# One merged loop for the HGRN2 layer: projections run in halves between the levels of the decay matrix

## What is computed

```
q, f_logit, i, g = split(rms_norm(h) @ w_in, 4)          # four 1024x1024 projections
f = lb + (1 - lb) * sigmoid(f_logit);  q = silu(q);  k = 1 - f;  v = i
b = cumsum(log f)
scores[t, s] = sum_k q[t,k] * exp(b[t,k] - b[s,k]) * k[s,k]      for s <= t
o = scores @ v      # in chunks with a running state in the reference, which is the same sum
h = h + (rms_norm(o, o_gain) * sigmoid(g)) @ w_out
```

## Time and profile before

| | us |
|---|---|
| median of 3 runs | 3078.87 |
| lowest, highest | 3076.29, 3081.34 |
| the profiled execution | 3075.35 |
| its span | 3073.6 |
| mean granted TensorE clock in the span | 0.969 |
| TensorE busy | 2937.2 (96%) |
| VectorE busy | 1462.0 (48%) |
| ScalarE busy | 1089.2 (35%) |
| GpSimd busy | 206.7 (7%) |

### The profile page before, as it was taken

How to read it: one execution, slowest core, us unless ns; L and a number is a source line. 1 busy time by engine, 2 the same in 40 slices (tenths; PEclk the granted TensorE clock), 3 DMA queues, 4 the chain that set the end, 5 groups by cost and what they waited for, 6 DMA issues and landing times.

```text
span 3073.6 us, 46468 instructions
## 1 busy us (share of the span) xinstructions
PE 2937.2 (96%) x17931; PEld 2548.8 (83%) x17931; DVE 1462.0 (48%) x2048; ACT 1089.2 (35%) x1717; POOL 206.7 (7%) x169
## 2 busy tenths in 40 slices
PE   8999999999999867799999999999999999799998
PEld 7877779999999866699988888887788887588887
DVE  5555545554344566555553444543533334544432
ACT  4333334333243443343332232332344444332222
POOL 1000000000000122210000110110100000200000
PEclk9999989999999877799999999999999999899999
DMA  4221213332343200033333323223211112233332
GB/s 124 52 61 49 61 42 95 90 89 83 95 121 89 61 1 0 0 90 95 89 92 94 104 69 93 78 71 89 83 49 48 48 48 73 65 96 94 90 94 71
DMA packets 419424, 225.54 MB, mean 73 GB/s; under 512 B 7461, under 2 KB 416294, under 8 KB 419222
## 3 DMA queue, kind: packets, MB, share of 16 engines
q1 hardware_dynamic: 416310, 211.45, 23.8%
q0 software_dynamic: 2256, 10.32, 1.1%
q10 hardware_dynamic: 784, 2.75, 0.3%
HBM read 222.36 MB, written 2.13 MB: 73 GB/s over the span
## 4 chain that ended last, share of the span: by engine, by line
PE 90%; DVE 5%; issue 2%; ACT 1%; POOL 1%; DVEq 0%; DMA 0%; ACTq 0%; POOLq 0%
PE ps L432 39%; PE ps L428 33%; PE ps L733 2%; PE ps L944 2%; PE ps L825 2%; PE ps L902 1%; PE ps L965 1%; PE ps L933 1%; PE ps L651 1%; PE ps L735 1%; PE ps L745 1%; PE ps L869 1%; PE ps L838 1%; PE ps L849 1%; PE ps L716 1%
## 5 line engine op out<-in xcount | busy, mean ns | idle before, releaser
L400 DVE TENSOR_TENSOR wl<-raw,wh 128x1024 fp32r<-128x1024 f32 (+2 forms) x421 | 512.9, 1218 | 437.6 <-ACT wh L396 434.1
L396 ACT ACTIVATE wh<-raw 128x1024 fp32r<-128x1024 f32 (+2 forms) x421 | 425.7, 1011 | 758.9 <-PE ps L428 395.4
L432 PE MATMUL ps<-xh,wh 128*128 128x264 f32 x2736 | 565.0, 288 | 7.3 <-DVE xl L461 5.5
L432 PE MATMUL ps<-xl,wh 128*128 128x264 f32 x2736 | 559.0, 286 | 0.0
L432 PE MATMUL ps<-xh,wl 128*128 128x264 f32 x2736 | 558.6, 286 | 0.0
L432 PEld LDWEIGHTS ps<-xh,wh 128*128 128x128 f32 x2736 | 428.5, 189 | 15.6 <-issue 4.1
L432 PEld LDWEIGHTS ps<-xl,wh 128*128 128x128 f32 x2736 | 426.1, 189 | 0.0
L432 PEld LDWEIGHTS ps<-xh,wl 128*128 128x128 f32 x2736 | 425.1, 189 | 0.0
L428 PE MATMUL ps<-xh,wh 128*128 128x512 f32 x976 | 392.3, 402 | 17.7 <-DVE xl L461 13.9
L428 PE MATMUL ps<-xl,wh 128*128 128x512 f32 x976 | 388.6, 398 | 0.0
L428 PE MATMUL ps<-xh,wl 128*128 128x512 f32 x976 | 386.4, 396 | 0.0
(11 more groups left out here) (295 smaller groups left out, 3915.7 us busy)
## 6 DMA issues: line engine op xcount, KB each, us to landing
raw<-in_w_in SPq DMA_DIRECT2D x88, 512.0 KB, 3.8
raw<-in_ffn_w_gate SPq DMA_DIRECT2D x44, 512.0 KB, 3.9
raw<-in_ffn_w_up SPq DMA_DIRECT2D x44, 512.0 KB, 3.8
raw<-in_w_ffn_in SPq DMA_DIRECT2D x44, 512.0 KB, 3.8
raw<-in_fox_w_in SPq DMA_DIRECT2D x33, 512.0 KB, 4.2
raw<-in_hgrn_w_in SPq DMA_DIRECT2D x32, 512.0 KB, 4.0
raw<-in_ffn_w_down SPq DMA_DIRECT2D x32, 448.0 KB, 3.5
raw<-in_ffn_w_down SPq DMA_DIRECT2D x16, 512.0 KB, 3.7
```

The source lines that it names most:

```text
L396: nc.scalar.activation(wh[:, v % 2, 0:nk, :], raw[:, v % RAW_SLOTS, 0:nk, :], ACT.Copy).then_inc(s("w_hi"), 1)
L400: nc.vector.tensor_tensor(wl[:, v % 2, 0:nk, :], raw[:, v % RAW_SLOTS, 0:nk, :], wh[:, v % 2, 0:nk, :].bitcast(F32), ALU.subtract).then_in ...
L432: last = nc.tensor.matmul(ps[:, bank + b, 0:HALF], w[:, slot, kk, :], x[:, k, b * HALF:(b + 1) * HALF], start=first, stop=end_)
```

## The change

Projections and heads become one loop over heads. A prologue of 3 groups (`PH_HGP`) projects f, q and v of head 0; the loop body of head i (`PH_HG`) projects f, q and v of head i+1 and the gate g of head i; the last body (`PH_HGL`) projects head 7's gate, and then does 8 groups of the output projection over the 6 heads that are done by then. `PH_HGOUT` keeps 8 groups over the last 2 heads, of 2 k tiles each. The dense groups of prologue and loop all use the one bank pair 0 and 1, the levels banks 2 and 3 in turn, the off-diagonal scores banks 4 and 5, outputs and the last 16 tokens 7 and 6.

A dense group is cut in two halves of 4 k tiles, and TensorE's order puts something between them or between groups. The diagonal comes first among the levels. Level buffers become three. All distances go to GpSimd. Sigmoids become -|x|, exp, ln(1+.), min and subtract, exp, so that ScalarE needs one table. Picks take only the later halves of the blocks (256 of 512 columns) from level 1 on, the last 16 tokens have their own small picks. `g_o` is no longer copied: the norm and the gate read bank 7.

```diff
-PH_HGRN = Phase(PH_DOWN0, HG_H, K8)
-PH_HGOUT = Phase(PH_HGRN, 2, K8)
+HG_BANKS = (0, 0)
+HG_EARLY = HG_H - 2
+PH_HGP = Phase(PH_DOWN0, 1, [[KT]] * 3, HG_BANKS)
+PH_HG = Phase(PH_HGP, HG_H - 1, K8, HG_BANKS)
+PH_HGL = Phase(PH_HG, 1, [[KT]] + [[HG_EARLY]] * KT, HG_BANKS)
+PH_HGOUT = Phase(PH_HGL, 2, [[KT - HG_EARLY]] * 4, (0, 2) if (PH_HGL.g0 + PH_HGL.gpi) % 2 else (2, 0))
...
     TensorE, body of head i
+        hgrn_level_mm(i, 0); hgrn_level_mm(i, 1)
+        half(0, 0)
+        hgrn_last_tokens(i)
+        if not first(i): hgrn_out(i - 1)
+        half(0, 1)
+        hgrn_level_mm(i, 2); hgrn_level_mm(i, 3)
+        half(1, 0)
+        if not first(i): hgrn_sum(i - 1, True)
+        half(1, 1)
+        hgrn_level_mm(i, 4); hgrn_level_mm(i, 5)
+        half(2, 0)
+        hgrn_off(i)
+        half(2, 1)
+        hgrn_level_mm(i, 6); hgrn_level_mm(i, 7)
+        half(3, 0)
+        if not last: ...; hgrn_turn(i + 1)
+        half(3, 1)
+        if last: hgrn_out(i); early(KT - 1); hgrn_sum(i, False)
...
     ScalarE, body of head i (not the last)
+            hgrn_exp(i, 1); hgrn_exp(i, 2); split(0)
+            if not first(i): sigmoid(o_e, i - 1, ...); hgrn_square(i - 1)
+            (copies of g_vt); hgrn_exp(i, 3..5)
+            act.wait_ge(s("psum_free"), evacuated(ph, n, 0)); below(f_x, f_e, "f_below", i + 1)
+            hgrn_exp(i, 6); split(1); sigmoid(f_e, ...); hgrn_rsqrt(i - 1); forget_log(i + 1)
+            act.wait_ge(s("psum_free"), evacuated(ph, n, 1)); below(q_x, q_e, "q_below", i + 1)
+            split(2); sigmoid(q_e, ...); hgrn_exp(i + 1, 0)
+            (copies of g_off); hgrn_hi(i - 1); hgrn_exps(i + 1); split(3)
+            act.wait_ge(s("psum_free"), evacuated(ph, n, 3)); below(o_x, o_e, "o_below", i)
...
     VectorE, body of head i (not the last)
+            hgrn_products(i, 1); hgrn_products(i, 2); split(0)
+            if not first(i): sigmoid_log(o_x, o_e, o_e, i - 1, "o_below", "o_logs")
+            hgrn_left(i)
+            if not first(i): hgrn_tail(i - 1)
+            pick(i, 0); pick(i, 1); scaled_out(ph, n, 0, f_x[:, :])
+            hgrn_products(i, 3); hgrn_products(i, 4); pick(i, 2); pick(i, 3)
+            sigmoid_log(f_x, ..., i + 1, ...); hgrn_products(i, 5); split(1)
+            forget(i + 1); scaled_out(ph, n, 1, q_x[:, :]); hgrn_running(i + 1)
+            hgrn_products(i, 6); pick(i, 4); pick(i, 5)
+            if not first(i): hgrn_out(i - 1)
+            sigmoid_log(q_x, ..., i + 1, ...); split(2); hgrn_stage(i + 1); scaled_out(ph, n, 2, g_v[:, :])
+            if not first(i): hgrn_lo(i - 1)
+            pick(i, 6); pick(i, 7); pick_last(i)
+            hgrn_products(i + 1, 0); split(3); scaled_out(ph, n, 3, o_x[:, :])
...
     VectorE, prologue
+        split_ahead(0); scaled_out(PH_HGP, 0, 0, f_x); split_ahead(1); sigmoid_log(f_x); scaled_out(PH_HGP, 0, 1, q_x)
+        forget(0); split_ahead(2); wait masks_loaded; tensor_copy(masks, masks_f); sigmoid_log(q_x)
+        hgrn_running(0); hgrn_stage(0); scaled_out(PH_HGP, 0, 2, g_v); hgrn_products(0, 0)
```

More of the change, by code:

```diff
@@ L243, in program @@
     g_f, g_lf, g_b = lnt, post_t[:, 0, :], post_t[:, 1, :]
[L244 to L254, removed]
+    g_r = ssq
     def ffn_area(n, at):
@@ L798, in _ @@
         feed_forward(0, PH_UP0, PH_DOWN0, 1, 1)
[L801 to L806, removed]
-                last = nc.tensor.matmul(ps[:, 4 + b, 0:HALF], mean_128, sq[:, 0, b * HALF:(b + 1) * HALF], start=True, stop=True)
-            last.then_inc(s("g_o_sum"), 1)
-        def hgrn(i):
-            pe.wait_ge(s("g_staged"), i + 1)
-            transposes(g_v, 4).then_inc(s("g_vt_mm"), 1)
[L813 to L830, removed]
-            pe.wait_ge(s("g_vt_ready"), i + 1)
[L832 to L844, removed]
@@ L861, in _ @@
+        pe.wait_ge(s("psum_free"), evacuated(PH_HGP, 0, 2))
+        pe.wait_ge(s("rstd_ready"), 3)
+        hgrn_turn(0)
+        hgrn(0)
+        loop(pe, HG_H - 1, hgrn, 1)
+        hgrn(HG_H - 1, True)
+        for i in range(2):
+            for gj in range(4):
+                pe_group(pe, PH_HGOUT, i, gj, yh, yl, ("y_ready", KT + HG_EARLY) if i + gj == 0 else None, HG_EARLY)
         feed_forward(1, PH_UP1, PH_DOWN1, 3, 3)
@@ L1746, in _, with sigmoid_log @@
-        loop(dve, HG_H, project)
-        dve.wait_ge(s("g_gates"), 2 * HG_H)
-        V.memset(g_diag[:, :], 0.0)
-        V.memset(g_k[:, L:NTT * P], 0.0)
-        dve.wait_ge(s("masks_loaded"), 16)
-        V.tensor_copy(masks[:, :, :], masks_f[:, :, :])
-        own(V.memset(g_qk[:, :, L:NTT * P], 0.0))
+        def sigmoid_log(x, e, out, n, below, done):
+            dve.wait_ge(s(below), 3 * n + 3)
+            V.scalar_tensor_tensor(out[:, :], x[:, :], 0.0, e[:, :], ALU.min, ALU.subtract).then_inc(s(done), 1)
@@ new lines, in pick @@
+        def pick(i, k):
+            dve.wait_ge(s("g_lv_mm"), (HG_LEVELS + 1) * i + k + 1)
+            if k == 0 and not first(i):
+                dve.wait_ge(s("g_o_mm"), i)
+            if k or not first(i):
+                dve.wait_ge(s("g_lv_used"), (HG_LEVELS + 1) * i + k)
+            if k:
+                width = hgrn_level(k - 1)[0]
+                dst, mask, src = (hgrn_halves(t, k - 1)[:, :, width:] for t in
+                                  (g_diag[:, 0:SEQ], masks[:, HG_LEVELS - k, 0:SEQ], ps[:, 2 + k % 2, :]))
+            else:
+                dst, mask, src = g_diag[:, 0:SEQ], masks[:, HG_LEVELS, 0:SEQ], ps[:, 2, :]
+            carry(dve, "dve_carry")
+            V.copy_predicated(dst, mask, src).then_inc(s("g_lv_used"), 1)
```

596 lines of the change are left out of this document (421 added, 175 removed).

## The result

| | before | after |
|---|---|---|
| time, median (lowest to highest) | 3078.63 us (3076.29 to 3081.34, 4 runs) | 2994.82 us (2991.50 to 2996.05, 4 runs) |
| profiled execution: time, span | 3075.35 us (time) | 2995.18 us, 2993.5 us |
| the layer: first product to the next layer's first | 489.0 us | 409.8 us |

The ratio is 0.9726, with a 95% interval from 0.9709 to 0.9743: faster, by 84 us in the medians. The forecast was 2993 us, 2989.7 for the profiled execution. The number came within 2 us; two of its terms were off by 7 and 12 us, and their errors partly cancelled.

A forecast was written before the change was run, and what follows sets the result against it. TensorE's work was taken to bound the merged loop at 41.2 us a head; 28.5 + 37.6 + 247.2 + 90 = 403.3 us against 489.0 gave 2989.7 profiled, 2993 median. Range 2974 to 3022, extended to 3030.

The forecast's parts named there:

- two of its terms: Six loop bodies at 41.2 us, 247.2 us; and last head to the next layer's first product, 90 us.
- TensorE's floor of 39.6 us: Loop, per head: 23.5 us of dense units and 16.1 of other TensorE work, which no instruction order undercuts.
- the body of 41.2: Loop body per head: 39.6 us plus 0.6 for operand changes and 1.0 of waiting; between 39.6 and 44.5.
- The wait at level 2: Loop, after group 3's end: TensorE waits about 1 us at level 2 for VectorE's diagonal pick.
- SBUF shared with GpSimd, +1.7 at most: Loop: GpSimd distances hold up VectorE products; only two in the tight stretch would show, +1.7 us a head.
- The start, 28.5: Layer's start to head 0's first transposes: 28.5 us, with TensorE losing 2.8 and idling 6 us.
- The last head, 54.6: Last head: its own work, the gate's unit, seven early groups and three evacuations with nothing between, 54.6 us.
- The end: Behind the last yl: seven steps of 3.0 us between short groups; 90 us from last head to next layer's first product.
- The sum: Layer: 28.5 + 37.6 + 247.2 + 90 = 403.3 us against 489.0, 85.7 less; median 2993 us.
- Rival (a), the order costs more: Loop: two more waits of 2.5 us a head, 40 in all; 3033 us, from 3028 to 3070; chance 0.11.
- Rival (b), the clock: Loop: stops at one bank pair keep TensorE's clock at 0.78, +90 us, 3083 us; chance 0.03.
- the early groups: Last head: eight early output groups, each 0.75 of a 5.88 us dense unit, 4.41 us.

The follow-up runs named there:

- Runs 5 and 6: Kernel after plus two extra VectorE multiplications in the first seven bodies: run 5 behind group 2's evacuation, 2991.92 us; run 6 behind `hgrn_left`, 3003.66 us.
- run 1: Kernel after, with ScalarE rounding the next unit's weights before it squares h, in the output projection only: 2986.48 us, ratio 0.9712.
- run 9: Kernel after, with the squares in the eight short output groups added up on VectorE, not GpSimd: 2990.93 us, ratio 0.9724.
- run 10: Kernel after, with eight whole output units, no early groups, and the cast of the masks on GpSimd: 2974.94 us, ratio 0.9670.
- run 7: Kernel after, with VectorE's cast of the masks moved behind head 0's first level products: 2995.48 us, one execution.
- run 4: Kernel after, with two level buffers instead of three and the last head's products 5 moved behind its early group 2: 3019.86 us, one execution.
- Run 2: Kernel after without early output groups; eight whole units of 8 k tiles follow the last head: 2976.10 us, ratio 0.9678.
- run 12: Kernel after, with four early, four whole, four short output groups, rounding before squaring, and the masks' cast on VectorE behind `forget`: 2975.82 us, ratio 0.9665.

## Why the prediction was right, and where it was not

Its mechanism held: TensorE bounds the merged loop, at clock 1.00, and one stretch of VectorE's order decides the little that is above the floor. By its steps:

- **TensorE's floor of 39.6 us** and the body of 41.2: measured 40.05. Floor and change-overs together were nearly right, 39.7 for 40.2: in the body from 967.51 the work besides the dense groups takes 15.1 for 16.1, and the dense halves with the changes around them 24.6 for 24.1. The wait at level 2 was 0.37 for 1.0. Runs 5 and 6 show that the right stretch was named.
- **SBUF shared with GpSimd, +1.7 at most:** two products of the tight stretch do take 1.21 and 1.28 us for 0.41 with a distance beside them, 1.7 in all, and TensorE still waits only 0.4 there, because the eight instructions of `hgrn_left` took 2.6 (0.56, 0.89 and 1.13) for the 3.8 worked out.
- **The start, 28.5:** measured 29.5. TensorE waits 2.21, 0.80 and 5.80 us there, for 2.8, 0.8 and 6 forecast. What the sum lacked is the low clock behind the first wait. From the evacuation of f to that of q it is 8.3 us in this profile and 6.9 in run 1's; here the group begins behind the 2.21 with records of 0.81 us, there with 0.51 (28.1 us from the first product to the transposes).
- **The last head, 54.6:** measured 57.2.
- **The end: this step failed.** The prediction had "a quarter split 0.35" in a step of 3.0 us. That split measured 1.50, because GpSimd's addition of squares holds it up, and the step is 4.0 to 4.8 (run 9 gives 0.42 back). Two of the seven steps have a split of 1024 columns in them besides, which the sum had none of. From the last yl on it is 31.1 us for 21; with 70.8 for 68.9 up to there, 102.0 for 90. It had weighed the same effect in the loop, where GpSimd computes distances, and not at the end, where GpSimd has another job. The Trainium skill, page "SBUF — State Buffer", section "SBUF: two separate sides", says that a VectorE instruction with two SBUF inputs and a GpSimd instruction that reads SBUF shut each other out, and that the one that starts first holds the other up for its whole length. The traces agree: 0.42 against 1.50 where GpSimd began 0.26 us earlier, run 10's 4.63, and 0.41 in run 1, where VectorE began 0.07 us earlier.
- **The low clock at the end was not in the sum either.** From the first short group to the next layer's first product TensorE is busy 20.0 of 31.1 us at clock 0.63:

```profile
1238.65:1269.77 31.12, 20.03 (x91) 18.18 (x91) 19.98 (x23) 12.31 (x21) 9.62 (x7) 0.63 0.27 80
```

  Here it costs little, as the step is set by VectorE's circle: in runs 5, 6 and 7, where the first records of this stretch ran at full clock (0.51 us for 0.81), the stretch takes 30.4.
- **The sum:** start and head 0 to level 0 of head 1 67.5 for 66.1, six bodies 240.3 for 247.2, last head and end 102.0 for 90: 409.8 us for 403.3. The profiled execution came to 2995.18, 5.5 over its 2989.7; the median of before stood 3.5 above its own profiled execution and lent the forecast those 3.5, while the median after lies 0.4 below its own. That the forecast hit the median within 2 us is in part this luck.
- **Rival (a), the order costs more,** was wrong for this kernel and right for its neighbour: with two buffers (run 4) four of the six bodies cost 3.8 more and two 2.2, by just such a circle. I had expected less than 1.5 us of that edit.
- **Rival (b), the clock:** in the loop it is 1.00, with waits of 0.37 us. At the end, where TensorE waits 1.0 to 2.3 us before each short group, it is 0.63. The Trainium skill, page "TensorE: Matmul & The Clock Gate", section "A second HAM failure mode: psum-queue depth-cycling", warns of clock swings from short idles between groups that cycle through PSUM; the trace agrees at the end and not in the loop, though it is the loop that has a single bank pair and the end that alternates between two.
- **What the prediction didn't ask:** it priced the early groups (4.4 each) and never what whole units would cost in their place. Run 2 shows that they would have been 21 us shorter in the trace.

## What to carry to other kernels

Work that is split to fill a gap must be priced against the cover that it takes away elsewhere: here k tiles moved into a head that hardly waited left eight groups too short to hide the hand-over behind them. Before a VectorE instruction with two SBUF inputs is costed by its mean, look at what GpSimd does in that very stretch; an idle GpSimd is no free place for work if VectorE is on the path beside it. And when a forecast comes out right, compare its terms all the same: this one was within 2 us with one term 7 us too high and another 12 too low.

## What the hardware showed that was not expected

- The pick with a mask (`copy_predicated`) of 256 columns takes 0.42 to 0.45 us for levels 0 to 4 and 0.73 to 0.74 for the two finest, whose columns come in runs of two and of one: as long as 512 columns in one piece (0.72 on average). Halving the columns bought nothing there.

```profile
960.24 0.73 DVE L1941 COPY_PREDICATED g_diag<-masks,ps 128x256 f32<-128x256 uint8 x1
961.47 0.74 DVE L1941 COPY_PREDICATED g_diag<-masks,ps 128x256 f32<-128x256 uint8 x1 [0.49 <-PE ps L854]
```

- GpSimd's cast of 4224 columns to bytes takes 3.71 us, VectorE's 2.35 alone (run 12) and 3.28 beside GpSimd's distances (run 7).
